# First input projection of a hybrid decoder step: one plain fp32 product in place of three split ones

## The reference, cut to what matters

```python
mod = jax.nn.silu(c) @ w_ada + b_ada
shift1, scale1, gate1, shift2, scale2, gate2 = jnp.split(mod[:, None, :], 6, axis=-1)
u = x * (1 + scale1) + shift1
proj = u @ w_in                      # 1024 x 4096
b_g, c_g, xa, xp, g_a, g_b = jnp.split(proj, SPLITS, axis=-1)
...
```

## Time and profile before

| | |
|---|---|
| median of 3 runs | 1340.86 us (1340.06 to 1345.46) |
| profiled execution, its own time | 1342.64 us |
| its span, first to last instruction | 1340.8 us |
| mean granted TensorE clock | 0.95 |
| PE busy | 1219.4 us, 91% of the span |
| DVE, ACT, POOL busy | 43%, 17%, 12% |
| first chunk: first matmul, end of the last | 46.47 us, about 78.3 us |

### The profile page before, as it was taken

The page is one execution under the profiler, slowest core; times in us unless marked ns, Lnnn a source line. Parts: engine busy times, 40 slices in busy tenths (PEclk is TensorE's granted clock), DMA queues, the critical chain, the costliest instruction groups (busy, mean ns, idle before and its releaser), DMA issues.

```text
span 1340.8 us, 17617 instructions
## 1 busy us (share of the span) xinstructions
PE 1219.4 (91%) x6231; PEld 528.0 (39%) x6232; DVE 573.2 (43%) x1062; ACT 233.7 (17%) x359; POOL 158.1 (12%) x94
## 2 busy tenths in 40 slices
PE   4599999957999999999999999999999999999980
PEld 0399965442333333333333333333333333333320
DVE  0814935684343333433333433434333433334346
ACT  0323310141121111111111111111111111112111
POOL 0546526047000000000000000000000000000003
PEclk8699999956999999999999999999999999999995
DMA  9733499572999999999996999999699999699941
GB/s 333 248 126 129 153 311 410 196 276 81 420 426 427 426 425 425 425 428 426 427 426 248 422 428 424 425 426 425 260 427 425 428 429 424 270 420 427 426 196 39
DMA packets 54708, 466.45 MB, mean 348 GB/s; under 512 B 5467, under 2 KB 5499, under 8 KB 18561
## 3 DMA queue, kind: packets, MB, share of 16 engines
q1 hardware_dynamic: 52817, 460.36, 83.4%
q0 software_dynamic: 1872, 5.84, 1.4%
HBM read 464.33 MB, written 1.85 MB: 348 GB/s over the span
## 4 chain that ended last, share of the span: by engine, by line
PE 63%; DMA 25%; DVE 9%; ACT 2%; issue 1%; SPq 1%; DVEq 0%; POOL 0%; ACTq 0%
PE bank L839 29%; DMA ring<-in_w_up 19%; PE bank L872 13%; PE bank L609 8%; PE bank L812 4%; PE bank L729 3%; DMA ring<-in_w_ada 3%; DMA hx<-in_x_sample 2%; PE bank L863 1%; ACT front L1002 1%; DMA mod_rows<-parts_home 1%; DVE u_low L1073 1%; PE bank L831 1%; PE bank L768 1%; PE bank L580 1%
## 5 line engine op out<-in xcount | busy, mean ns | idle before, releaser
L839 PE MATMUL bank<-ring,front 128*64 128x512 f32 x2240 | 506.9, 598 | 15.2 <-DMA ring<-in_w_up 15.0
L839 PEld LDWEIGHTS bank<-ring,front 128*64 128x64 f32 x2240 | 150.8, 137 | 315.1 <-issue 284.5
L872 PE MATMUL bank<-ring,front 128*64 128x512 f32 x1120 | 248.0, 595 | 7.3 <-ACT front L1002 7.3
L1285 DVE TENSOR_TENSOR front<-front,bank 128x512 f32<-128x512 f32 (+1 forms) x210 | 143.8, 685 | 84.5 <-PE bank L812 71.9
L872 PEld LDWEIGHTS bank<-ring,front 128*64 128x64 f32 x1120 | 77.3, 137 | 153.9 <-issue 139.9
L1329 DVE TENSOR_TENSOR O_low<-bank,O_high 128x512 fp32r<-128x512 f32 x35 | 24.2, 692 | 244.3 <-ACT O_high L1005 244.3
L999 ACT ACTIVATE front<-front 128x256 f32<-128x256 f32 x70 | 29.2, 417 | 546.0 <-DVE front L1303 546.0
L533 POOL TENSOR_TENSOR parts_home<-parts_home,front 128x1024 f32<-128x1024 f32 x2 | 4.7, 2374 | 991.5 <-ACT parts_home L934 991.5
L1303 DVE TENSOR_SCALAR front<-bank 128x256 f32<-128x256 f32 x70 | 29.7, 425 | 155.8 <-PE bank L839 154.5
L609 PE MATMUL bank<-u_high,ring_parts 128*128 128x320 f32 x512 | 80.7, 316 | 9.5 <-ACT u_high L894 5.7
L454 POOL TENSOR_TENSOR ring_parts<-ring,ring_parts 128x1024 fp32r<-128x1024 f32 x32 | 77.6, 2455 | 80.9 <-ACT ring_parts L905 80.9
(11 more groups left out here) (215 smaller groups left out, 942.3 us busy)
## 6 DMA issues: line engine op xcount, KB each, us to landing
ring<-in_w_up SPq DMA_DIRECT2D x128, 2048.0 KB, 17.5
ring<-in_w_down SPq DMA_DIRECT2D x128, 1024.0 KB, 16.8
ring<-in_w_ada SPq DMA_DIRECT2D x12, 2048.0 KB, 15.5
ring<-in_w_in SPq DMA_DIRECT2D x8, 2048.0 KB, 12.9
ring<-in_w_o SPq DMA_DIRECT2D x2, 2048.0 KB, 19.5
hx<-in_x_prompt SPq DMA_DIRECT2D x2, 1024.0 KB, 23.8
ring<-in_w_out_a SPq DMA_DIRECT2D x1, 2048.0 KB, 7.5
ring<-in_w_out_b SPq DMA_DIRECT2D x1, 2048.0 KB, 14.9
```

What stands on the lines that cost most here:

```text
L839: last = mm(bank[B_UP[j]][64 * h:64 * h + 64, :], x_T[:, (c % 2) * 2 + b, 64 * (c // 2):64 * (c // 2) + 64], w[:, :, at:at + 256], start=F ...
L872: last = mm(bank[B_DOWN][64 * h:64 * h + 64, :], act_T[:, 2 * j + b, 64 * hh:64 * hh + 64], expert_chunk_at(UP_CHUNKS + m)[:, b * 1024 + h ...
L1285: signal(TT(Y[0:r, 2 * t + h, :], Y[0:r, 2 * t + h, :], bank[b][0:r, :], ALU.add), bank_free[b], value)
```

## The change

The first chunk (`IN_ORDER[0]`, blocks `proj4` to `proj7`) is computed by a new function `proj_plain`: plain fp32 matmuls of the raw weights in their slot by `u_T` itself. The block of rows k is the outermost loop, with the four output blocks inside, so work on block k can start when `u_T[:, k, :]` is written. Nothing of this chunk is split: four of ScalarE's copies and four of GpSimd's subtractions go. ScalarE writes all of `u_high` first and then splits the second chunk. Because `u_low` overwrites `u_T`, VectorE now waits on a new semaphore `u_read` (and for the last block on `proj7`) before each L1073. The counts of `w_high_ready` and `w_low_ready` start one chunk later, and ScalarE's guard of the high slots covers the second and third chunk.

```diff
-            for i in range(8):
+            for i in range(1, 8):
                 slot = front_slot(IN_CHUNK + i)
                 for q in range(4):
-                    pool.wait_ge(w_high_ready, 4 * i + q + 1)
+                    pool.wait_ge(w_high_ready, 4 * (i - 1) + q + 1)
...
+            def proj_plain(m4):
+
+                w = chunk(IN_CHUNK).rearrange("p (k m) -> p k m", k=KC)
+                blocks = [take(f"proj{4 * m4 + j}") for j in range(4)]
+                for k in range(KC):
+                    wait_read(pe, f"x_T{k}")
+                    for j in range(4):
+                        last = mm(blocks[j][:, 0:NT], w[:, k, j * P:(j + 1) * P], u_T[:, k, :], start=k == 0, stop=k == KC - 1)
+                        if k == KC - 1:
+                            done(f"proj{4 * m4 + j}", last)
+                    if k < KC - 1:
+                        last.then_inc(u_read, 1)
...
-                            pe.wait_ge(w_high_ready, 4 * i + k // 2 + 1)
-                        if i == 0 and j == 0:
+                            pe.wait_ge(w_high_ready, 4 * (i - 1) + k // 2 + 1)
+                        if i == 1 and j == 0:
                             pe.wait_ge(u_high_ready, k + 1)
...
-            proj(0, IN_ORDER[0])
+            proj_plain(IN_ORDER[0])
...
-            def split_high(i, between=lambda q: None):
+            def split_high(i):
...
-                if i < 2:
-                    wait_chunk_read(act, HIGH_SLOT[i])
+                if i <= 2:
+                    wait_chunk_read(act, HIGH_SLOT[i % 2])
...
-            split_high(0, between=lambda q: [high_of_u(k) for k in (2 * q, 2 * q + 1)])
+            for k in range(KC):
+                high_of_u(k)
             split_high(1)
...
             for k in range(KC):
                 dve.wait_ge(u_high_ready, k + 1)
+                if k < KC - 1:
+                    dve.wait_ge(u_read, k + 1)
+                else:
+                    wait_full(dve, f"proj{4 * IN_ORDER[0] + 3}")
                 signal(TT(u_low[:, k, :], u_T[:, k, :], u_high[:, k, :].bitcast(F32), ALU.subtract), u_low_ready, k + 1)
```

## The result

The changed kernel takes 1328.09 us (median of 4, 1326.51 to 1329.61) against 1341.24 us of the kernel before (median of 4): 0.9897 of the time, 95% interval 0.9885 to 0.991, 13.15 us less. In a second set beside other kernels it was 1327.98 against 1341.98, ratio 0.9899 (0.9884 to 0.9913), 14.0 us less. Forecast were 13.9 us less and 1327.0 us.

The account below looks back on a forecast made before the run. Bound near the change: TensorE waiting for late u_T and u_low, and low clock. Start 44.75 + matmuls 17.4 + clock 2.2 = 64.35 against 78.23, 13.9 us earlier; taken from the median 1340.86: 1327.0 us, range 1323.5 to 1332.5.

Parts of the forecast that it names:

- Start of the plain chunk: First chunk's first plain matmul, released when the bank of x_T3 is read: about 44.75 us, against 46.47 before.
- Plain matmul: First chunk: 0.544 us each at full clock, taken from L662, so 17.4 us for the chunk's 32.
- that rival, 9.3 us: Plain chunk: weight loads or bank changes show, costing 9.3 us, leaving a gain of 4.6, 1336.2 us; chance 0.05.
- Clock: TensorE starts the plain chunk at clock 0.50 and rises to 1.00 under it: adds 2.2 us (0.2 to 2.85).
- c: Length in us of the plain chunk's stretch at clock 0.50, which adds c/2: 4.4, bounds 0.4 and 5.7.
- the rival on the slow side: Plain chunk: the clock does not rise under it, giving 1344.4 or 1356.3 us; chance 0.04.
- The sum: Start, plain matmuls and clock put the histories' transposes at 64.35 us instead of 78.23: 13.9 us earlier.
- Covers: Work removed, added or moved around the first chunks stays hidden: u_low by 3 us at least, banks 0 to 0.5 us.
- the meeting of VectorE and GpSimd: First chunk: the engines running side by side stretch L1070 from 0.23 to 1.99 us and the last u_low to 2.53.
- the mark: Start of the histories' transposes behind the first chunk, at 78.23 us before, from which the change is measured.

Follow-up runs that it names:

- e3: The changed kernel, each PSUM bank asked for right before its first matmul, in the order banks come free: 1327.04 us, ratio 0.9885.
- e11: e3 again, the changed kernel asking for banks as needed, in a later set: 1326.68 us, ratio 0.9887.
- e5: The changed kernel with the second chunk of the projection also in plain fp32: 1333.47 us, ratio 0.9937.
- e8: e5 with VectorE's two copies of the histories placed ahead of the u_low instructions: 1330.23 us, ratio 0.9919.
- e0: The changed kernel once more, unedited, as yardstick in a second set: 1327.98 us, ratio 0.9899.
- e1: The changed kernel with the output block as outermost loop and the block of rows inside: 1329.1 us, ratio 0.9905.
- e6: e3 plus 14 throwaway warm-up matmuls in TensorE's waits for the first w_ada chunks, before x lands: 1326.1 us, ratio 0.988.
- e4: The changed kernel with four throwaway GpSimd subtractions put back while VectorE writes u_T: 1330.32 us, ratio 0.9913.
- e2: The kernel before, GpSimd starting all its subtractions only when VectorE has written all of u_low: 1331.52 us, ratio 0.9927.
- e7: The kernel before, GpSimd starting its subtractions when all of u_T is written, not waiting for u_low: 1343.18 us, ratio 1.0006.
- e9: The kernel before, only the second chunk's GpSimd subtractions waiting until u_low is written: 1334.06 us, ratio 0.9947.
- e10: e6 plus one throwaway matmul ahead of each block's transposes of x, eight more: 1325.27 us, ratio 0.987.

## Why the prediction was right, point by point

- **Start of the plain chunk.** 44.75 forecast; 46.10 measured, 44.93 with the later landing taken off. The bank of `x_T3` did release it, 0.35 us after it was read where I had taken 0.18. e3 and e11 show that the bank, not `u_T` or the weights, set the start.
- **Plain matmul.** 0.544 us taken from L662. From 51 to 65 PE is busy without a gap, and the whole chunk to L649, 19.42 us, is 17.4 plus half of the 4.1 us at 0.50. e5's second plain chunk, all at 1.00, took 17.40. Four banks in turn cost nothing that shows; that rival, 9.3 us, is ruled out.
- **Clock.** c of 4.4 (0.4 to 5.7) forecast; 4.1 measured. In the other profiles it was 3.0 (e5), 3.1 (e8), 4.3 (e0), 4.7 (e1), 4.8 (e3), 4.9 (e6), 5.2 (e11) and 5.7 (e4): the range held, and that its middle lay within 0.3 us of this profile's 4.1 is partly luck. One reading was off: the row that gave 3.0 us ends at 58.4, and the clock rose near 58.8, 3.4 us after 55.40. Where it was low at the start it rose under the plain chunk in every profile, so the rival on the slow side fell.
- **The sum.** 13.9 us forecast, 13.9 from the first transpose of `x`, 13.15 and 14.0 in medians. Right, with no term off by more than 0.4 us. That the two 13.9 agree to a tenth is luck: e0, a profile of the same kernel, gives 15.6 by the same count, since the clock stood at 1.00 during its transposes.
- **Covers.** `u_low` was wanted at 71.04 and its last ended at 66.22: covered. The banks of `proj4` and `proj5` were free in time: the second chunk began 0.74 us behind L649, as before. The seven chunks and the wait for `w_ada` were unchanged, so nothing was tied to absolute time.
- **Where my account was thin.** I named the meeting of VectorE and GpSimd as "part of" why the end came at 78.23. Taking it away alone shortens the interval by 11.5 us where the change brings 13.9 (e2), and the larger share came from the second chunk's subtractions, which the change keeps. The forecast did not need to know, since it was made from the new order alone; but a reader would have drawn from it that the plain product is what pays. e2 gets 10.5 us without it.
- **The half-known part.** The span fell 14.2 us and the mark 12.7. The other 1.5 us lie behind the mark, where one instruction alone was 1.8 us shorter (below). No step of mine speaks of it, and the runs do not tie it to the change: over the profiles with at most one plain chunk the span behind the mark goes from 1260.2 to 1263.5 us, and before (1262.6) and after (1261.1) both lie within. That the profiles' 14.2 comes so near the forecast is thus luck, within a microsecond or two.

## What to carry to other kernels

When a short VectorE instruction shows several times its own length, look which GpSimd instruction runs beside it, for which stage that one works, and whether it can start later: one semaphore wait brought 10.5 us here (e2), and shifting it to the wrong place nothing (e7). A reformulation that drops the dependence altogether is dearer in TensorE time (17.4 as against 14.1 us a chunk) and pays only where the parts are waited for (e5, e8). And before a wait is lengthened, read what is queued behind it on that engine: two small copies cost e5 a stand of 1.9 us and, in its profile, a fall of the clock.

## What was not expected of the hardware

One instruction in the norm, far behind the change, was 1.8 us shorter in the profile after. Before, and after (timeline, start and us):

```profile
272.06 2.12 POOL L494 TENSOR_TENSOR front<-front,parts_home 128x1024 f32<-128x1024 f32 x1 [49.95 <-ACT parts_home L951]
272.27 2.46 DVE L1172 SCALAR_TENSOR_TENSOR hx<-hx,front 128x512 f32<-128x512 f32 x1
```

```profile
259.44 0.69 DVE L1190 SCALAR_TENSOR_TENSOR hx<-hx,front 128x512 f32<-128x512 f32 x1
259.47 2.65 POOL L495 TENSOR_TENSOR front<-front,parts_home 128x1024 f32<-128x1024 f32 x1 [51.96 <-ACT parts_home L965]
```

VectorE's instruction takes 2.46 us when GpSimd's began 0.21 us before it, and 0.69 us when it began 0.03 us before GpSimd's, which is then the longer one (2.65 as against 2.12). In these rows who starts first keeps about its own time, and the other waits. The change does not decide it. The instruction took 0.69 us in seven profiles (the changed kernel, e0, e2, e6, e8, e9, e10) and 1.78 to 2.46 us in the other seven (the kernel before, e1, e3, e4, e5, e7, e11), and both forms of the first chunk stand on both sides. So differences of one or two microseconds between two of these kernels may come from this pair.

The Trainium skill, SBUF — State Buffer, section Who interferes with whom, says that the port pair shared by the two engines is an exclusive lock and that "Issue order, not op shape, decides who blocks"; the pair of rows agrees. By it a VectorE instruction whose other input comes from PSUM does not meet GpSimd, and in e4 L1097, of that kind, stays at 0.22 to 0.23 us beside GpSimd while L1098 behind it takes 1.43 to 1.48.

The clock fell during transposes even when it had been 1.00 as they began (e1, e3, e6, e7, and e10's profile with dense matmuls between them). In e0 it stayed at 1.00 through all of them, 33.94 to 39.66 us, and fell only at 40.1, in the gap before the plain chunk. What would hold it there is open.
